# A decoder layer on one core: split weights and normed tensor laid a whole number of 2 KB rows apart, and the scale rows spread between the first residuals

## The reference

```python
mod = silu(c) @ w_ada + b_ada                      # 6 vectors of 1024
shift1, scale1, gate1, shift2, scale2, gate2 = split(mod, 6)

h = rms_norm(x, norm1_g) * (1 + scale1) + shift1
q, k, v, qi, ki, wi, u_pool, g_attn, g_pool = split_cols(h @ w_in)
attn = dsa_sparse_attention(rms_norm(q), rms_norm(k), v, qi, ki, wi)   # top 128 keys, 8 heads of 64
y_attn = attn @ w_attn_br
y_pool = multiscale_pool(u_pool, w_pool_grp, pool_scale) @ w_pool_br
merged = sigmoid(g_attn) * y_attn + sigmoid(g_pool) * y_pool
x = x + gate1 * (merged @ w_out)

h2 = rms_norm(x, norm2_g) * (1 + scale2) + shift2
up = h2 @ w_up                                     # 1024 x 5632
y = conv_b + causal_depthwise_conv(up, conv_w)     # width 3
a, b = split(y, 2)
x = x + gate2 * ((silu(a) * b) @ w_down)           # 2816 x 1024
```

## Time and profile before

| | |
|---|---|
| median of 3 runs | 755.13 us (753.65 to 755.42) |
| the profiled execution | 754.11 us |
| its span, first to last instruction | 751.2 us |
| TensorE busy | 732.7 us (98% of the span) |
| VectorE, ScalarE, GpSimd busy | 385.2, 307.6, 300.6 us |
| mean granted TensorE clock | 0.994 of full |
| HBM traffic | 92.1 MB |
| share of the last chain on TensorE | 95% |

### The profile page before, as it was taken

The page is one execution under the profiler, slowest core; times in us unless marked ns, Lnnn a source line. Parts: engine busy times, 40 slices in busy tenths (PEclk is TensorE's granted clock), DMA queues, the critical chain, the costliest instruction groups (busy, mean ns, idle before and its releaser), DMA issues.

```text
span 751.2 us, 9512 instructions
## 1 busy us (share of the span) xinstructions
PE 732.7 (98%) x3536; PEld 582.7 (78%) x3536; DVE 385.2 (51%) x706; ACT 307.6 (41%) x507; POOL 300.6 (40%) x159
## 2 busy tenths in 40 slices
PE   5899999999999999999899999999999999999997
PEld 3667688877777778888698888887888888888886
DVE  3458999944455517699855445555434432004002
ACT  6325532576567633341645343343344343121120
POOL 1001548735232335474316444344334434444340
PEclk9899999999999999999999999999999999999999
DMA  9991412211221237394095234234234133142401
GB/s 320 389 389 57 127 57 74 95 57 57 92 78 57 63 111 263 136 314 150 1 332 145 61 108 113 68 101 113 57 112 111 59 110 112 31 149 74 140 0 56
DMA packets 87307, 92.74 MB, mean 123 GB/s; under 512 B 2275, under 2 KB 69599, under 8 KB 87263
## 3 DMA queue, kind: packets, MB, share of 16 engines
q1 hardware_dynamic: 84927, 83.23, 34.3%
q10 hardware_dynamic: 2336, 8.92, 3.1%
HBM read 90.05 MB, written 2.10 MB: 123 GB/s over the span
## 4 chain that ended last, share of the span: by engine, by line
PE 95%; DVE 2%; DMA 1%; SPq 1%; ACT 1%; issue 1%; ACTq 0%; DVEq 0%
PE bank L1562 38%; PE bank L1582 24%; PE bank L1571 19%; PE bank L1632 5%; PE bank L1809 1%; PE bank L1831 1%; PE bank L1797 1%; DMA ada_first<-in_w_ada_dram 1%; PE bank L1614 1%; PE bank L1693 1%; PE bank L1866 1%; PE bank L1672 0%; PE bank L1622 0%; PE bank L1663 0%; DVE tmp_last L1453 0%
## 5 line engine op out<-in xcount | busy, mean ns | idle before, releaser
L697 POOL TENSOR_TENSOR wsplit<-stage,wsplit 128x1024 fp32r<-128x1024 f32 (+1 forms) x113 | 258.1, 2286 | 401.4 <-ACT wsplit L781 338.3
L1562 PE MATMUL bank<-hT,wsplit 128*128 128x512 f32 (+1 forms) x1120 | 263.0, 387 | 0.0
L1562 PEld LDWEIGHTS bank<-hT,wsplit 128*128 128x128 f32 x1120 | 203.7, 188 | 46.0 <-issue 1.7
L781 ACT ACTIVATE wsplit<-stage 128x1024 fp32r<-128x1024 f32 (+2 forms) x121 | 120.1, 994 | 262.5 <-PE bank L1571 174.8
L1571 PE MATMUL bank<-hT,wsplit 128*128 128x512 f32 (+1 forms) x560 | 137.3, 387 | 0.0
L1582 PE MATMUL bank<-wsplit,guT 128*128 128x512 f32 x528 | 123.4, 395 | 0.0
L1571 PEld LDWEIGHTS bank<-hT,wsplit 128*128 128x128 f32 x560 | 101.6, 188 | 22.4 <-POOL wsplit L697 0.3
L1582 PEld LDWEIGHTS bank<-wsplit,guT 128*128 128x128 f32 x528 | 99.1, 188 | 24.1
L1520 DVE SCALAR_TENSOR_TENSOR yb<-bank,conv,yb 128x511 f32<-128x511 f32 (+1 forms) x44 | 33.0, 749 | 67.4 <-ACT yb L1100 66.6
L1520 DVE SCALAR_TENSOR_TENSOR ya<-bank,conv,ya 128x511 f32<-128x511 f32 (+1 forms) x44 | 33.0, 750 | 62.4 <-ACT ya L1100 61.6
L1453 DVE TENSOR_TENSOR tmp_last<-bank,gate_row 128x512 f32<-128x512 f32 x8 | 5.5, 688 | 105.0 <-PE bank L1582 105.0
(11 more groups left out here) (193 smaller groups left out, 765.5 us busy)
## 6 DMA issues: line engine op xcount, KB each, us to landing
stage<-in_w_up_dram SPq DMA_DIRECT2D x44, 512.0 KB, 5.2
stage<-in_w_in_dram SPq DMA_DIRECT2D x14, 1024.0 KB, 5.2
stage<-in_w_down_dram SPq DMA_DIRECT2D x10, 1024.0 KB, 5.0
ada_first<-in_w_ada_dram SPq DMA_DIRECT2D x16, 512.0 KB, 8.4
ada_mid<-in_w_ada_dram ACTq DMA_DIRECT2D x8, 1024.0 KB, 6.9
ada_row<-in_w_ada_dram SPq DMA_DIRECT2D x8, 512.0 KB, 10.5
stage<-in_w_out_dram SPq DMA_DIRECT2D x4, 1024.0 KB, 6.8
ada_last<-in_w_ada_dram SPq DMA_DIRECT2D x4, 1024.0 KB, 10.3
```

The source lines that it names most:

```text
L697: pool.tensor_tensor(unit_split(n, 1), unit_source(n), unit_split(n, 0).bitcast(F32), ALU.subtract).then_inc(low, 1)
L781: me.did(act.activation(unit_split(n, 0), unit_source(n), ACT.Copy), high)
L1562: pe.matmul(out_bank[:, tokens], hi[:, k, :], rhs[:, part, k, tokens], start=k == 0 and part == 0, stop=False)
```

## The change

`hT` is put at the next offset that lies a whole number of 2,048-byte rows behind `wsplit`, where it was at the next multiple of 128; `halves` (128 bytes) moves from ahead of it into the arena. By the sizes, `hT` is then at 86,144 and the arena starts 128 bytes lower than before; the distance from `wsplit` to `hT` is 53,248 bytes, 26 rows. No other tensor changes its place in the arena, and no matmul, transfer or elementwise instruction is added or removed.

The order on three engines changes. VectorE: `gate_vector(0)` after three scale rows instead of five, and the other five between the residuals, sums and inverse of tiles 0; `mod_vector(4)` behind `wo_residual(1, 1)`. TensorE: `mod_columns(4)` behind `x2_turn(0)` instead of behind tile 0 of half 1. ScalarE: the high parts of the first two up units behind `scaled(0)`, together with the third; and `scaled(0)` waits for six scale rows instead of eight.

```diff
+        split_at = at[0]
         wsplit = place("wsplit", [P, NRING, 2, WU], F32R)
...
-        halves = place("halves", [P, 32], F32)
...
-        at[0] += -at[0] % P
+        at[0] += (split_at - at[0]) % (4 * S)
         hT_at = at[0]
         hT = place("hT", [P, 2, KD, S], F32R)
...
-        assert base + 107 * K1 + 32 <= nc.sbuf_usable_end, (base, nc.sbuf_usable_end)
+        assert base + 107 * K1 + 192 <= nc.sbuf_usable_end, (base, nc.sbuf_usable_end)
...
+        halves = arena("halves", [P, 32], F32, 107.0625)
...
                 if t == 0:
-                    act.wait_ge(mod_sum, KD * (ROW_TURN[4] + 1))
+                    act.wait_ge(mod_sum, KD * ROW_TURN[4] + 6)
...
                 square_half(0, t)
-            high_parts(sch.unit["ua", 1])
             square_half(1, 0)
...
-            for k in range(5):
+            for k in range(3):
                 mod_row_of(4, k)
             gate_vector(0)
             me.settle()
-            for k in range(5, KD):
-                mod_row_of(4, k)
...
-            for t in range(NT):
-                if t == 2:
-                    mod_vector(4)
-                wo_residual(0, t)
+            wo_residual(0, 0)
+            mod_row_of(4, 3)
+            wo_residual(0, 1)
+            wo_residual(0, 2)
+            mod_row_of(4, 4)
+            wo_residual(0, 3)
...
             wo_residual(1, 0)
+            mod_row_of(4, 5)
             token_sum(0)
+            mod_row_of(4, 6)
             token_inverse(0)
+            mod_row_of(4, 7)
             for t in (1, 2):
                 wo_residual(1, t)
+                if t == 1:
+                    mod_vector(4)
+                    me.settle()
                 h2_full(t - 1, 0)
...
-                if t == 0:
+                if t == 1:
+                    x2_turn(0)
                     pe.wait_ge(gate_ok, 2)
                     mod_columns(4)
-                if t == 1:
-                    x2_turn(0)
```

## The result

The changed kernel takes 737.35 us (median of 4 runs, 737.13 to 737.66) against 755.11 us (753.65 to 755.42) before: ratio 0.9769, 95% interval 0.9752 to 0.9786, or 17.8 us less. The profiled execution took 737.66 us, with a span of 735.6 us, 15.6 us shorter than before, at a mean granted clock of 0.997 (before 0.994). The forecast was 737.5 us.

What follows compares the result with a forecast made beforehand. TensorE, busy 732.7 of 751.2 us, was taken as the bound. Layout 15.1 us plus order 1.8 us, 16.9 us off the profiled 754.11, gave 737.2, stated as 737.5 us; range 734.5 to 753.5.

Steps and rivals of the forecast that it cites:

- The inference the forecast hung on: 512-column products: row distance between operands, not place, makes `own` faster, 226.7 against 233.2 ns; layout worth 15.1 us.
- Whole rows: Products with `wsplit`: operands a whole number of 2,048-byte rows apart were to bring all 2,628 to 226.7 ns.
- Rival A: Products with `wsplit`: layout changes nothing, `own` is faster for another reason; only the order's 1.8 us remain, 752.3 us; 22%.
- Rival B: Lines 1562, 1571, 1632: whole-row distance is dearer with stationary weights, 1.6 ns at 512 columns; 755.5 to 758.5 us; 8%.
- Its price at 256 columns: The 144 matmuls of 256 columns using `wsplit`: 0.8 ns dearer each at whole-row distance, 0.1 us.
- 5.7 ns for each of 1,572 matmuls: Products outside the output projection and the second part of up and down: from 232.4 to 226.7 ns each, 9.0 us.
- The 0.7 us for VectorE's top-key chain: Before 150 us: VectorE's top-key search keeps its length, so 0.7 us of TensorE's saving is lost, bounds 0 and 2.7.
- The sign that the prediction named: Sign of a wrong forecast: faster pace with new TensorE waits between 60 and 165 us, VectorE's top-key chain setting that part.
- The prediction's last step, from 737.2 to 737.5: Whole kernel: 737.2 us raised to 737.5 because the profiled execution lay 1.0 us below the median of three.
- 2.4 - 0.6: Output projection to first up unit: order cuts the `xs` wait from 3.04 to 0.6 us, less 0.6 new wait: 1.8 us.
- the `h2_low(1)` wait: Ahead of the first up unit: `h2_low(1)` comes later after the transposes, 0.6 us of new wait.

Runs made afterwards that it cites:

- layout alone: The kernel before with only the changes to the offset of `hT`, `halves` and the arena's bound, order of work as before: 740.61 us against 755.26, ratio 0.981.
- the order alone: The kernel before with only the reordered work on the three engines, all places as before: 751.15 us, ratio 0.9946.
- X = 64: The changed kernel with `hT` and the arena moved 64 bytes further from `wsplit`: 744.28 us, against 756.61 for the kernel before.

## Why the prediction came out

- **The inference the forecast hung on held:** distance, not place, makes `own` faster. The up and down projections gave 5.8 + 3.5 us for 5.9 + 3.5, branch products 1.1 for 1.1. The stage up to the first attention score gave 2.4 for 2.2, but by luck: 0.9 of it was the clock, and the layout's share 1.5. "Whole rows" was narrower than what the chip asks: 256 bytes.
- **Rival A** (layout worth nothing, 752.3 us) falls by layout alone at 740.61. The rule behind it, in the Trainium skill's SBUF — State Buffer (Who interferes with whom), that TensorE's reads never wait on anyone, may hold between engines; it doesn't cover TensorE's own two operands, where the distance between their addresses alone changes 226.7 into 233.3 ns.
- **Rival B** (stationary weights in step dearer) falls: line 1567 runs at 226.7. Its price at 256 columns is real (1.2 ns where 0.8 was taken; the stage took 0.3 us more instead of 0.1), but doesn't carry over to 512.
- **Mis-sized: short runs.** One price, 5.7 ns for each of 1,572 matmuls, was taken from runs of hundreds and used on short ones too. In attention (runs of 4 to 16) it missed 1.1 us. Ahead of it the runs of 35 and 56 went from 232.4 to 226.7 ns, but those of 6 and 7 didn't gain (231.7 ns before and 233.9 after for 7): of 516 x 5.7 = 2.9 us some 0.8 never came, beside the waits of the next point.
- **The 0.7 us for VectorE's top-key chain** were sized well: a `kiT` wait of 0.5 us where 0.2 stood, and 0.3 us for `kraw`, 0.6 us in all. The sign that the prediction named, VectorE's chain setting that part, came about too, without making the forecast wrong.
- **The closeness of 737.5 is in part chance.** The span was to shrink by 16.9 us and shrank by 15.6. The start's +1.0 us, not from the change, and the clock's 0.9 us cancel; what is left is 1.8 us missed up to the branch products (0.7 and 1.1), made good in part by 0.8 us more from the order. The rest came from outside the mechanism: 0.9 us outside the span, and the two profiled executions' places beside their medians. The prediction's last step, from 737.2 to 737.5, has no working: all of the 1.0 us that it names would have given 738.2.
- **Mis-sized: the order.** 2.4 - 0.6 was worked out; the idle time went from 3.04 to 0 and 0.42 came new, 2.6 us (2.7 with the order alone; its medians say more, with 1.8 outside the interval). VectorE's and ScalarE's timelines of the changed kernel show where:

```profile
348.04 0.69 DVE L1453 TENSOR_TENSOR xtok<-tmp,xtok 128x512 f32<-128x512 f32 x1
...
349.84 0.15 DVE L1472 TENSOR_TENSOR tstat<-tstat 128x1 f32<-128x1 f32 x1
...
355.19 0.17 DVE L1176 TENSOR_TENSOR mod<-bank,vec 128x8 f32<-128x8 f32 x1 [1.23 <-PE bank L1668]
```
```profile
351.42 1.34 ACT L1067 ACTIVATE xs<-xtok,tstat 128x512 f32<-128x512 f32 x2 [1.10 <-DVE tstat L1477]
```

From the output projection's start, which came 3.30 us earlier, the residual (1,0) ends at 352.0 in the prediction's time frame (352.3 worked out there), the sum starts at 353.1 (353.7) and half 0 of `xs` is done at 355.4 instead of 356.1. TensorE is through tile 1 at 355.6, exactly as worked out, so the two now meet without a wait. `mod_vector(4)` stands 1.23 us on the narrow matmuls, as foreseen, and the `h2_low(1)` wait was foreseen at 0.6 us and is 0.42.

## What to carry to other kernels

Compare stretches of one shape, at the same granted clock, by start-to-start time, never by the mean duration of a row, and look for an operand that makes the difference; here 6.6 ns in 233 were worth 2% of the kernel, on an engine that is 98% busy. For matmuls of this kind (512 columns of `float32r`, each with its own weight load) place the two operands a whole number of 256 bytes apart, and price such a gain by the length of the run that it falls in. Look at the chain of the changed kernel too: a stage that gains may have come to hang on another engine. Put work that the next turn needs ahead of work that has slack, and follow the chain to what is late next: a new wait of 0.4 us was part of the price.

## What the runs showed of the hardware

- A 512-column product with its weight load takes 226.7 ns when the stationary and the moving operand are 0, 256 or 512 bytes (modulo 2,048) apart, and 228.9 to 234.3 ns at the other distances tried (32, 64, 96, 128, 160, 192 and 224 modulo 256); the sign of the distance counts at 64. For 256 columns the best distance seen is another one, X = 64, that is 192 for stationary less moving (113.3 ns against 120.0), so one layout doesn't serve both sizes best.
- After an interruption TensorE comes back to 226.7 ns only after some ten products (223 to 236 on the way; about 314 for the first one behind a break). A transpose of 128 columns in the middle of a run costs about 0.14 us in all: the up projection took 11.7 us more for 84.
- TensorE's granted clock was at half for 2.8 to 5.6 us behind the first product with `hT` in every kernel profiled, and once again, with layout alone, behind a wait of 3.13 us; before, a wait of 3.04 us left it at full. A us at half cost about 0.5 us, an estimate from the lengths of the stage up to attention.
- What inside the chip makes the distance count was not settled. A conflict between the reads of the two operands would fit a period of 256 bytes, but no run here shows it directly.
